# First block of the first projection: one row tile of x loaded and multiplied ahead of the other

## The reference, cut to what matters

```python
def hybrid_layer(x, norm_g, w_in, ...):
    hn = rmsnorm(x, norm_g)                       # x / sqrt(mean(x*x) + eps) * norm_g
    proj = jnp.einsum('bsd,dc->bsc', hn, w_in)    # 2048 -> 12292 columns
    br = proj[..., :QKVG_COLS].reshape(b, s, N_BRANCH, 4, BRANCH_W)
    ...
```

## Time and profile before

| | us |
|---|---|
| median of 3 runs | 2105.65 |
| runs, lowest to highest | 2104.89 to 2108.10 |
| the profiled execution, its own time | 2105.61 |
| its span, first to last instruction | 2103.8 |
| TensorE busy | 2059.6 |
| VectorE busy | 1659.8 |
| ScalarE busy | 1046.6 |
| mean granted TensorE clock, of full speed | 0.994 |

### The profile page before, as it was taken

How to read it: one execution, slowest core, us unless ns; L and a number is a source line. 1 busy time by engine, 2 the same in 40 slices (tenths; PEclk the granted TensorE clock), 3 DMA queues, 4 the chain that set the end, 5 groups by cost and what they waited for, 6 DMA issues and landing times.

```text
span 2103.8 us, 27194 instructions
## 1 busy us (share of the span) xinstructions
PE 2059.6 (98%) x10029; PEld 1723.1 (82%) x10029; DVE 1659.8 (79%) x2444; ACT 1046.6 (50%) x1353; POOL 124.3 (6%) x187
## 2 busy tenths in 40 slices
PE   7999999999999999999999999899999999999998
PEld 6877788888887878787888888788888888878886
DVE  6889989878888887787666786578999999875554
ACT  5555445644444545446335554455555555544443
POOL 0010100100011111011000000000000000100000
PEclk9999999999999999999999999999999999999999
DMA  8798888788998999896444347567778777667664
GB/s 302 262 295 259 272 282 270 236 269 273 349 347 299 333 328 355 303 312 188 134 130 122 110 132 245 181 188 243 233 228 262 235 229 223 204 218 234 195 191 140
DMA packets 287423, 505.64 MB, mean 240 GB/s; under 512 B 22907, under 2 KB 114529, under 8 KB 285265
## 3 DMA queue, kind: packets, MB, share of 16 engines
q1 hardware_dynamic: 276320, 468.77, 67.7%
q0 software_dynamic: 10992, 35.45, 6.1%
HBM read 489.45 MB, written 23.88 MB: 244 GB/s over the span
## 4 chain that ended last, share of the span: by engine, by line
PE 51%; DVE 1%; DMA 1%; ACT 0%; issue 0%; ACTq 0%; DVEq 0%
PE gemm_ps L2042 24%; PE gemm_ps L2538 8%; PE ps L2538 7%; PE gemm_ps L2543 4%; PE ps L2543 4%; PE ps L2392 1%; PE ps L2461 1%; DMA w_raw<-in_w_out_dram 1%; DVE w_lo L1208 0%; PE ps L2415 0%; PE ps L2414 0%; PE ps L2375 0%; PE ps L2358 0%; PE ps L2092 0%; PE ps L2339 0%
## 5 line engine op out<-in xcount | busy, mean ns | idle before, releaser
L1208 DVE TENSOR_TENSOR w_lo<-w_raw,w_hi 128x1024 fp32r<-128x1024 f32 (+1 forms) x688 | 831.0, 1215 | 303.7 <-ACT w_hi L758 300.4
L758 ACT ACTIVATE w_hi<-w_raw 128x1024 fp32r<-128x1024 f32 (+1 forms) x688 | 716.9, 1053 | 611.2 <-PE gemm_ps L2042 224.0
L2042 PE MATMUL gemm_ps<-w_hi,a_both 128*128 128x512 f32 x2944 | 953.0, 397 | 13.3 <-DVE w_lo L1208 7.0
L2042 PEld LDWEIGHTS gemm_ps<-w_hi,a_both 128*128 128x128 f32 x2944 | 554.7, 188 | 141.4 <-DVE w_lo L1208 10.7
L2042 PE MATMUL gemm_ps<-w_lo,a_both 128*128 128x512 f32 x1472 | 575.2, 391 | 0.0
L2042 PEld LDWEIGHTS gemm_ps<-w_lo,a_both 128*128 128x128 f32 x1472 | 277.8, 189 | 54.8 <-issue 1.0
L2538 PE MATMUL gemm_ps<-a_both,w_hi 128*128 128x512 f32 x704 | 178.7, 396 | 1.7 <-DVE a_both L1248 1.6
L2538 PE MATMUL ps<-a_both,w_hi 128*128 128x512 f32 x672 | 169.0, 392 | 0.0
L1947 DVE SCALAR_TENSOR_TENSOR acc<-gp,cw,acc 128x256 f32<-128x256 f32 x344 | 151.6, 481 | 7.7 <-ACT acc L1157 3.7
L2538 PEld LDWEIGHTS gemm_ps<-a_both,w_hi 128*128 128x128 f32 x704 | 127.5, 190 | 25.3 <-DVE a_both L1248 2.3
L2538 PEld LDWEIGHTS ps<-a_both,w_hi 128*128 128x128 f32 x672 | 120.6, 189 | 21.3
(11 more groups left out here) (448 smaller groups left out, 1862.1 us busy)
## 6 DMA issues: line engine op xcount, KB each, us to landing
w_raw<-in_w_in_dram SPq DMA_DIRECT2D x336, 512.0 KB, 4.6
w_raw<-in_w_up_dram SPq DMA_DIRECT2D x336, 256.0 KB, 3.3
mraw<-in_w_mod_dram SPq DMA_DIRECT2D x160, 512.0 KB, 5.9
w_raw<-in_w_down_dram SPq DMA_DIRECT2D x84, 512.0 KB, 4.3
w_raw<-in_w_out_dram SPq DMA_DIRECT2D x64, 512.0 KB, 5.5
mraw_ffn<-in_w_mod_dram SPq DMA_DIRECT2D x32, 512.0 KB, 4.8
w_raw<-in_w_up_dram SPq DMA_DIRECT2D x24, 512.0 KB, 5.4
fold_d<-msum POOLq DMA_DIRECT2D x9, 512.0 KB, 7.0
```

What stands on the lines that cost most here:

```text
L758: act.activation(w_hi[:, slot, :, 0:n], raw[:, slot, :, 0:n], ACT.Copy).then_inc(hi_done, 1)
L1208: dve.tensor_tensor(w_lo[:, slot, :, 0:n], raw[:, slot, :, 0:n], w_hi[:, slot, :, 0:n].bitcast(F32), ALU.subtract).then_inc(lo_done, 1)
L2042: mm = pe.matmul(out[:, rt, 0:n], x[:, chunk0 + k, rt * P:(rt + 1) * P], w[:, slot, kk, 0:n], start=(k == 0 and part == 0), stop=(k == chu ...
```

## The change

It does five things at the beginning of the program.

1. SP loads row tile 0 of x, weight units 0 and 1, row tile 1, and then units 2 and 3.
2. TensorE transposes four chunks of one row tile at a time (turn_tile, two groups for each tile, still four transposes a group), multiplies units 0 to 3 with tile 0 alone (6 matmuls a unit), then the same four units with tile 1, and units 4 to 7 with both tiles as before. Groups 4 to 7 are turned as before; groups 4 and 5 behind units 1 and 3 of tile 1, groups 6 and 7 behind units 4 and 5.
3. DVE and ACT work on x for units 0 to 3 in four pieces of one tile and four chunks (128x512), DVE with one tensor_tensor against a broadcast norm_g in place of two tensor_scalar.
4. For units 4 to 7, ACT makes a_hi of group i and then w_hi of unit i, and DVE makes `whole` of group i, w_lo of unit i, then a_lo of group i.
5. row_squares of tile 0 stands behind w_hi of unit 5, of tile 1 behind that of unit 8; condition() behind that of unit 7; small_vectors is cut in three parts, behind a_lo of groups 4, 5 and 6.

The diff, cut to its core:

```diff
-            for rt in range(RT):
-                sp.dma_start(x_sb[:, rt], xv[:, rt]).then_inc(S(f"x_in{rt}"), 16)
-            units(w_in, 0, 0, count=SLOTS)
+            sp.dma_start(x_sb[:, 0], xv[:, 0]).then_inc(S("x_in0"), 16)
+            units(w_in, 0, 0, count=2)
+            sp.dma_start(x_sb[:, 1], xv[:, 1]).then_inc(S("x_in1"), 16)
+            units(w_in, 0, 0, first=2, count=SLOTS - 2, row=2 * UK)
...
-            row_squares(0)
+            def turned_tile(rt, g):
+
+                act.wait_ge(S("tr_val"), 2 * rt + g + 1)
+                own = slice(rt * P, (rt + 1) * P)
+                act.activation(a_hi[:, 4 * g:4 * g + 4, own], whole[:, 4 * g:4 * g + 4, own], ACT.Copy).then_inc(S("tr_hi"), 1)
+
             splits(0, 0, 1)
-            turned("x", 0)
+            turned_tile(0, 0)
             splits(0, 1, 2)
+            splits(0, 2, 3)
+            turned_tile(0, 1)
+            splits(0, 3, 4)
+            turned_tile(1, 0)
+            turned_tile(1, 1)
...
-                    for i in range(2, 10):
-
-                        if B == 0 and i > 2:
-                            turned("x", i - 2)
+                    for i in range(4 if B == 0 else 2, 10):
+
+                        if B == 0 and i < 8:
+                            turned("x", i)
                         splits(2 * B, i, i + 1)
...
-                        if (B, i) == (0, 4):
-                            row_squares(1)
-                        if (B, i) == (0, 6):
+                        if B == 0 and i in (5, 8):
+                            row_squares((i - 5) // 3)
+                        if (B, i) == (0, 7):
                             condition()
...
-            turned("x", 0, vec[:, 0:16])
+            def turned_tile(rt, g):
+
+                dve.wait_ge(S("tr_ps"), 2 * rt + g + 1)
+                gain = vec[:, 4 * g:4 * g + 4].unsqueeze(2).to_broadcast([P, 4, P])
+                dve.tensor_tensor(whole[:, 4 * g:4 * g + 4, rt * P:(rt + 1) * P], ps[:, g].rearrange("p (k t) -> p k t", k=4),
+                                  gain, ALU.mult).then_inc(S("tr_val"), 1)
...
+            turned_tile(0, 0)
             splits(0, 0, 1)
-            turned_rest("x", 0)
+            turned_tile_rest(0, 0)
             splits(0, 1, 2)
+            turned_tile(0, 1)
+            splits(0, 2, 3)
+            turned_tile_rest(0, 1)
+            turned_tile(1, 0)
+            splits(0, 3, 4)
+            turned_tile_rest(1, 0)
+            turned_tile(1, 1)
+            turned_tile_rest(1, 1)
...
-                        if B == 0:
-                            if i > 2:
-                                turned_rest("x", i - 2)
-                            if i < 9:
-                                turned("x", i - 1, vec[:, 0:16])
+                        if B == 0 and i < 8:
+                            turned("x", i, vec[:, 0:16])
                         splits(2 * B, i, i + 1)
-                        if (B, i) == (0, 4):
-                            small_vectors()
+                        if B == 0 and i < 8:
+                            turned_rest("x", i)
+                        if B == 0 and 4 <= i < 7:
+                            small_vectors(i - 4)
...
+                pe.wait_ge(S("x_in0"), 16)
+                for g in range(2):
+                    turn_tile(0, g)
+                for i in range(SLOTS):
+                    unit(i, (0,), i // 2 + 1)
+                    if i == 0:
+                        pe.wait_ge(S("x_in1"), 16)
+                        turn_tile(1, 0)
+                    if i == 2:
+                        turn_tile(1, 1)
+                for i in range(SLOTS):
+                    unit(i, (1,), 2 + i // 2 + 1).then_inc(used, 1)
+                    if i == 1:
+                        pe.wait_ge(S("vec_in"), 144)
+                        pe.transpose(pC[:, 0:88], vrows[0:88, :], ident[0:88, 0:88]).then_inc(S("n_vecT"), 1)
+                    if i in (1, 3):
+                        turn("x", x_sb, 0, 4 + i // 2)
+                for i in range(SLOTS, BU):
+                    unit(i, (0, 1), i + 1).then_inc(used, 1)
+                    if i < SLOTS + 2:
+                        turn("x", x_sb, 0, i + 2)
+                    forget_gates(0, i)
```

More of the change, by code:

```diff
@@ L1460, in masked_biases, with turned_tile_rest @@
                 me(masked(forget_bias[:, :, P:T], 0))
-            turned("x", 0, vec[:, 0:16])
+            def turned_tile(rt, g):
[3 more added lines that the diff above has]
+                                  gain, ALU.mult).then_inc(S("tr_val"), 1)
+            def turned_tile_rest(rt, g):
+                dve.wait_ge(S("tr_hi"), 2 * rt + g + 1)
+                chunks, own = slice(4 * g, 4 * g + 4), slice(rt * P, (rt + 1) * P)
+                dve.tensor_tensor(a_lo[:, chunks, own], whole[:, chunks, own], a_hi[:, chunks, own].bitcast(F32),
+                                  ALU.subtract).then_inc(S("tr_lo"), 1)
+            turned_tile(0, 0)
             splits(0, 0, 1)
-            turned_rest("x", 0)
+            turned_tile_rest(0, 0)
             splits(0, 1, 2)
+            turned_tile(0, 1)
[6 more added lines that the diff above has]
+            turned_tile_rest(1, 1)
             for seg in range(4):
@@ L2200, in _, with turn_tile, first_block, unit @@
             pe.transpose(pC[:, 96:112], gain0[:, :], ident[0:16, 0:16]).then_inc(S("n_vecT"), 1)
-            for rt in range(RT):
-                pe.wait_ge(S(f"x_in{rt}"), 16)
+            def turn_tile(rt, g):
+                if rt:
+                    pe.wait_ge(S("tr_val"), 2 * rt + g - 1)
+                for k in range(4):
+                    mm = pe.transpose(ps[:, g, k * P:(k + 1) * P], x_sb[:, rt, (4 * g + k) * P:(4 * g + k + 1) * P], ident)
+                mm.then_inc(S("tr_ps"), 1)
+            def first_block():
+                def unit(i, tiles, turned):
+                    pe.wait_ge(S("tr_lo"), turned)
+                    pe.wait_ge(lo_done, i + 1)
+                    for kk in range(UK):
+                        k = UK * i + kk
+                        for rt in tiles:
+                            for part, (x, w) in enumerate(((a_hi, w_hi), (a_hi, w_lo), (a_lo, w_hi))):
+                                mm = pe.matmul(gemm_ps[:, 0, rt], x[:, k, rt * P:(rt + 1) * P], w[:, i % SLOTS, kk],
+                                               start=(k == 0 and part == 0), stop=(k == KC - 1 and part == 2))
+                    return mm
+                pe.wait_ge(S("x_in0"), 16)
[20 more added lines that the diff above has]
+                    forget_gates(0, i)
+            first_block()
             for seg in range(4):
@@ L2216, in after @@
                             forget_gates(B, u)
-                    product(BU * B, 0, B % 2, a_hi, a_lo, BU, after=after,
-                            turning=("x", x_sb, 0) if B == 0 else None)
+                    if B:
+                        product(BU * B, 0, B % 2, a_hi, a_lo, BU, after=after)
             pe.wait_ge(S("h_ylo"), HEADS)
```

30 lines of the change are left out of this document (15 added, 15 removed).

## The result

| | us |
|---|---|
| kernel before, median of 8 runs | 2106.22 (2104.89 to 2109.08) |
| changed kernel, median of 8 runs | 2112.01 (2110.14 to 2114.29) |
| ratio, with its 95% interval | 1.0023 [1.0014, 1.0031] |
| the same as a difference | +4.9 [+3.0, +6.5] |
| the profiled execution of the change | 2110.77, span 2109.0 |

What follows compares the result with a forecast made beforehand. TensorE, busy 98% of the span, was taken as the bound, so unit 8's shift carries to the end: -2.55 start, -1.2 old waits, +6.8 new waits, -0.3 unit lengths, +2.75 on 2105.65, giving 2108.4 us; range 2105.6 to 2111.0.

Steps and rivals of the forecast that it cites:

- The start: Loads and first tile: the first matmul comes at 11.0 instead of 13.57, 2.55 us earlier.
- the 408 GB/s that I had counted with: Early loads: transfer rate read from the trace, giving 1.29 us for each weight unit.
- The rival of the early bytes: Start: early loads usable no sooner, first matmul stays at 13.5; +5.2 us, 2110.9; chance 5%.
- The chain: Units 4 to 7: VectorE and ScalarE pieces run serially, 4.27 us a unit against TensorE's 3.2; unit 8 starts 2.75 later.
- the clock in the gaps: Units 4 to 7: TensorE's waits drop its clock to 1.2 GHz; +7.9 us, 2113.5; rival, chance 5%.
- the main case: Whole kernel: early start spent by waits before units 4 to 7, total 2108.4 us; chance 66%.
- The base: Whole kernel: the median before, 2105.65 us, to which the forecast shift was added.
- the sum: Shift of unit 8's start: -2.55 start, -1.2 old waits, +6.8 new waits, -0.3 unit lengths; together +2.75 us.
- The covered chain: Units 4 to 7 keep TensorE's 3.2 us a unit; -4.1 us, 2101.5; rival, chance 7%.

Runs made afterwards that it cites:

- the first trace: The changed kernel's first profiled execution: 2110.77 us, unit 8 starting at 45.73.
- the three traces of before: Three profiled executions of the unchanged kernel, the prediction's own and two repeats: 2105.61, 2107.18 and 2106.70 us.
- the four of the change: Four profiled executions of the changed kernel, the first and three repeats; unit 8 started at 45.73, 46.66, 46.04 and 44.66 us.
- before_serial: Kernel before, with only the change's order of pieces for units 4 to 7; 2113.22 us, ratio 1.0029 to before.
- w_hi_first: Changed kernel, each engine making the weight's piece first in units 4 to 7 (w_hi before a_hi, w_lo before `whole`); 2106.72 us, ratio 1.0000 to before.
- small_in_gap: Changed kernel, the three small-vector parts moved from behind a_lo to between `whole` and w_lo; 2108.11 us, ratio 1.0006 to before.
- overlapped2: Changed kernel with neighbouring units' work overlapped, w_hi and w_lo of units 8 and 9 behind group 7's a_hi and a_lo; 2103.68 us, ratio 0.9990 to before.
- after_again: Changed kernel unaltered, traced again and timed on another chip; 2111.52 us, ratio 1.0022 to before.
- after_third: Changed kernel unaltered, one more execution for its trace; 2111.13 us.
- old_load_order: Changed kernel, both tiles of x loaded ahead of the weights again; 2115.12 us, ratio 1.0044 to before.
- the fourth trace of the change: Changed kernel unaltered, the last of its repeat executions for a trace; 2107.92 us.
- overlapped: Changed kernel, weight pieces made one unit (VectorE) and two units (ScalarE) ahead of x pieces, first squares and small vectors earlier; 2105.84 us, ratio 0.9997 to before.
- fill_gap: Changed kernel, extra unread transposes of x on TensorE filling its waits around units 4 to 7; 2109.72 us, ratio 1.0016 to before.

## Why the prediction was wrong

**The start was right, 0.4 us off.** -2.55 was forecast and -2.12 measured in the first trace (11.45 against 13.57); in the others the first matmul is at 11.52, 11.01 and 11.11. w_hi of unit 0 started at 8.48, not 8.05, in the first trace, but at 8.04 and 8.14 in the last two. The stretch of 4 to 8 us in the change (columns as in the earlier trace rows) moved less than the 408 GB/s that I had counted with:

```profile
4.00:8.00 4.00, 1.38 (x7) 1.38 (x8) 0.15 (x1) 0.00 (x0) 0.00 (x0) 1.00 0.98 384
```

At 384 unit 0 would take 1.37 us in place of 1.29, so the rate explains 0.1 of the 0.4; the rest isn't explained. The Trainium skill ("DMA: Bandwidth & Descriptors", Specifications) gives 358 GB/s; all four traces of the change lie above it, at 384 to 399. The rival of the early bytes fell with this instant. The clock rose at 17.4 in the first trace, where I took 16.5, and sooner in the other three. By the 25th matmul the three traces of before have a mean of 22.40 and the four of the change 19.90, so 2.5 us were won on average.

**The chain was right in kind and size.** Forecast from the turn to tile 1 (20.1) to unit 8 (45.25): 25.15 us (the forecast's own terms add up to 45.22). Measured where the clock holds: 25.09 and 25.12. Forecast rounds of 4.27 and the small vectors; measured 4.26 to 4.28 with them taken off; the small vectors 1.58 together, forecast 1.61. The waits before units 4 to 7 were forecast at 1.5, 1.4, 1.5 and 2.4, measured 1.24, 1.12, 1.06 and 2.24. before_serial, w_hi_first, small_in_gap and overlapped2 move this stretch to 26.0, 22.8, 23.6 and 18.8 by the order of the pieces (in the first, 0.8 is the clock's). Nothing else of the change cost anything that a trace shows: the tensor_tensor out of PSUM took 0.69 (I took 0.8), the table load and squares hold nobody back.

**The step that failed, as far as the runs show one, is the clock in the gaps.** I called it a rival with 5%, priced at 7.9 us with all four units at the low level, and argued against it from the one wait of 1.03 us in the trace of before. Both the chance and the price were wrong. In the first block of all these traces no wait of 0.25 to 1.69 us was followed by a falling clock, while behind the eight waits of 2.07 to 2.41 us it fell five times (after_again, after_third, before_serial, old_load_order, w_hi_first; not in the first and the fourth trace of the change nor in overlapped). A row of a wait half as long says nothing of the longer one. And it fell for about 3 us, then rose again, at 1.5 us for a unit of the change: a small loss in a part of the executions, which belongs into the main case as a term of about +0.8 (two of four), not beside it as an unlikely 7.9. With that term the forecast would have been 2109.2, and the range's upper end, with the whole 1.5, 2112.5. So the term alone doesn't take the forecast out of its range: of the 3.6 us between 2108.4 and 2112.0 it is 0.8, the base is 0.6, what the traces lose after unit 8 is 0.4, and 1.8 stays open. The Trainium skill ("TensorE: Matmul & The Clock Gate", A second HAM failure mode) tells of short idling between groups that makes the clock swing; two of the four traces of this program agree, behind a wait of 2.2 us, and two do not. I had set the rule aside on a row that did not test it.

**The base was taken from one execution.** The prediction measured everything against a trace and a median of three runs. The median of eight was 2106.22, 0.57 above; and from unit 8 to the end that trace was the quickest of the three.

The account by means of the traces: -2.5 to the 25th matmul; +5.2 for the chain; +0.8 for the clock (two falls of 1.5 in four); +0.4 after unit 8, which is within the scatter of either kernel. Together +3.9, the difference of the mean spans (2108.6 less 2104.7). The timed runs say +4.9 by the ratio, within 3.0 and 6.5, and +5.8 and +5.0 by the medians of the two comparisons. The last 1 to 2 us aren't settled. They seem to belong to the change itself: against before, the medians of before_serial, fill_gap, small_in_gap, w_hi_first and both overlapped kernels differ by what the start of unit 8 in their one trace says, to within 0.6 us, while the change is 2.0 to 2.8 above that and old_load_order, which has the same four waits, 1.5. The fourth trace (2107.92) lies under all twenty timed runs of the change, so the traces may hold more undisturbed executions than the timed runs do. A fall of the clock in every execution would add only 0.8, and the record can't show it: the mean granted clock of an execution is there to three places, 0.994 to 0.996 in both kernels, and was 0.994 for the first trace without a fall and 0.995 for after_again with one.

**Sign and size.** The direction was right, and the cause of its larger part. But I held a change within 0.2% for the likeliest (76%), and the measured 4.9 us lies beyond 4.2, by less than its own uncertainty. The +2.75 of the sum is two terms that the runs bear out, -2.5 and +5.2; what the sum lacks is only in part accounted for. The covered chain (7%) did not come; only overlapped2 comes near to it.

## What to carry to other kernels

When two engines hand pieces to each other inside a round, write the round as a chain before moving anything: if each engine makes only the pieces of one group, the handovers add up, and a piece of the next group that needs nothing from this one belongs into the hole (1.65 us here), as long as it doesn't itself wait for a load. Four passes that begin 2.5 us sooner are worth nothing if the units behind them come 1.4 us apart more than TensorE needs. And a wait of TensorE has to be priced with what the clock may do after it; where it is longer than any wait in the trace of before, that trace cannot rule the fall out.

## What was not expected of the hardware

- The clock fell from 2.4 to 1.2 GHz behind single waits of 2.07 to 2.41 us in five cases of eight, for six to eight matmuls (about 3 us; granted clock 0.50), though TensorE had run at the high level since 20 us or sooner with only shorter waits between. In w_hi_first it was the only wait. Behind those of 0.25 to 1.69 us in the first block it never fell.
- The same start gave a 25th matmul at 21.81, 22.57 and 22.81 in one kernel and at 19.44 to 20.64 in the other: of these spreads of 1.0 and 1.2 us the instant at which the clock rises makes 1.0 in the first kernel (first to 25th matmul 8.32 to 9.36) and 0.8 in the second (8.43 to 9.19), about a fifth of the whole effect.
- One tensor_tensor of 128x512 out of PSUM against a broadcast operand took 0.69 us, as long as the same shape in SBUF (0.68) and less than the two tensor_scalar out of PSUM (0.88).
